# Latent attention in groups of two head columns, with its norms on GpSimd, in a two-block transformer kernel

## The reference, cut to what matters

```python
cq, ckv, kr, qd, kd, vd = _split(h @ w_in, CD_SIZES)
q = (rms_norm_2(cq, g_cq) @ w_uq).reshape(B, S, C_HEADS, C_NOPE + C_ROPE)   # 8 heads, 64 + 32
q_nope, q_rope = jnp.split(q, [C_NOPE], axis=-1)
q_rope = apply_rope_2(q_rope, ang_c)
kv = (rms_norm_2(ckv, g_ckv) @ w_ukv).reshape(B, S, C_HEADS, C_NOPE + C_V)
k_nope, v_c = jnp.split(kv, [C_NOPE], axis=-1)
k_rope = apply_rope_2(kr.reshape(B, S, 1, C_ROPE), ang_c)                   # one for all heads
qc = jnp.concatenate([q_nope, q_rope], axis=-1)[:, :, :, None, :]
kc = jnp.concatenate([k_nope, jnp.broadcast_to(k_rope, (B, S, C_HEADS, C_ROPE))], axis=-1)
oc = blocked_dense_attention(qc, kc, v_c, (C_NOPE + C_ROPE) ** -0.5)
...
s = jnp.einsum('bqhgd,bkhd->bhgqk', q_blk, k) * scale      # blocked_dense_attention, 128 queries a block
p = jax.nn.softmax(s, axis=-1)
return jnp.einsum('bhgqk,bkhd->bqhgd', p, v)
```

## Time and profile before

| what | value |
|---|---|
| median of 3 runs | 2272.75 us (2271.89 to 2274.1) |
| the profiled execution: its span | 2275.0 us |
| the profiled execution: its own run time | not given |
| instructions | 33281 |
| TensorE busy | 2199.9 us |
| VectorE busy | 1246.9 us |
| ScalarE busy | 1078.0 us |
| GpSimd busy | 853.7 us |

### The profile page before, as it was taken

One profiled execution on the slowest core, in us unless ns is written; L12 is line 12 of the kernel. 1 busy time (PEld: TensorE's weight loads), 2 busy tenths in 40 slices (PEclk: granted clock), 3 DMA queues, 4 the chain that ended last, 5 costly groups with the idle time before them and its releaser, 6 DMA issues.

```text
span 2275.0 us, 33281 instructions
## 1 busy us (share of the span) xinstructions
PE 2199.9 (97%) x12130; PEld 1763.7 (78%) x12130; DVE 1246.9 (55%) x2614; ACT 1078.0 (47%) x2160; POOL 853.7 (38%) x665
## 2 busy tenths in 40 slices
PE   8999899999999999989999999999999999999997
PEld 6778667888866788668888888888767888888886
DVE  6997782499778446885552112234666655211222
ACT  6542484465247652685453223343566545322332
POOL 4333304443330343104255545554110425554553
PEclk9999899999999999999999999999999999999998
DMA  5334002332410233203233333343110323333331
GB/s 171 85 91 141 25 2 79 104 91 79 144 38 11 75 89 109 68 2 110 67 94 96 95 109 98 92 124 95 48 60 20 111 66 97 94 95 100 98 96 66
DMA packets 107186, 189.74 MB, mean 83 GB/s; under 512 B 12049, under 2 KB 22801, under 8 KB 106897
## 3 DMA queue, kind: packets, MB, share of 16 engines
q1 hardware_dynamic: 101136, 178.67, 27.3%
q10 hardware_dynamic: 5888, 8.95, 1.2%
HBM read 182.85 MB, written 2.10 MB: 81 GB/s over the span
## 4 chain that ended last, share of the span: by engine, by line
PE 85%; DVE 10%; issue 3%; ACT 2%; POOL 1%; DMA 0%; SPq 0%; DVEq 0%; ACTq 0%
PE bank L861 23%; PE bank L863 23%; PE bank L862 23%; PE bank L1090 3%; PE bank L1103 3%; PE bank L1076 2%; DVE temp L1933 1%; DVE bank L2053 1%; PE bank L868 1%; DVE temp L1965 1%; PE bank L1067 1%; PE bank L1070 1%; PE bank L931 1%; DVE temp L1967 1%; POOL w_lo L2212 1%
## 5 line engine op out<-in xcount | busy, mean ns | idle before, releaser
L2212 POOL TENSOR_TENSOR w_lo<-w_raw,w_hi 128x512 fp32r<-128x512 f32 (+3 forms) x618 | 824.7, 1341 | 1337.1 <-ACT w_hi L1226 1336.7
L861 PE MATMUL bank<-op_hi,w_hi 128*128 128x512 f32 x1840 | 734.4, 399 | 9.1 <-POOL w_lo L2212 4.4
L863 PE MATMUL bank<-op_hi,w_lo 128*128 128x512 f32 x1840 | 719.4, 391 | 0.0
L862 PE MATMUL bank<-op_lo,w_hi 128*128 128x512 f32 x1840 | 719.4, 391 | 0.0
L1226 ACT ACTIVATE w_hi<-w_raw 128x512 fp32r<-128x512 f32 (+2 forms) x634 | 385.4, 617 | 682.5 <-PE bank L863 678.8
L861 PEld LDWEIGHTS bank<-op_hi,w_hi 128*128 128x128 f32 x1840 | 347.1, 189 | 95.7 <-issue 15.3
L862 PEld LDWEIGHTS bank<-op_lo,w_hi 128*128 128x128 f32 x1840 | 347.6, 189 | 73.4 <-issue 4.1
L863 PEld LDWEIGHTS bank<-op_hi,w_lo 128*128 128x128 f32 x1840 | 347.1, 189 | 73.7
L1648 DVE TENSOR_TENSOR temp<-bank,rstd 128x512 f32<-128x512 f32 x151 | 104.4, 691 | 396.0 <-PE bank L863 378.2
L861 PE MATMUL bank<-side_hi,w_hi 128*128 128x512 f32 (+1 forms) x628 | 233.2, 371 | 2.5 <-DVE side_lo L1730 1.4
L863 PE MATMUL bank<-side_hi,w_lo 128*128 128x512 f32 (+1 forms) x628 | 230.9, 368 | 0.0
(11 more groups left out here) (269 smaller groups left out, 2256.3 us busy)
## 6 DMA issues: line engine op xcount, KB each, us to landing
w_raw<-in_weights SPq DMA_DIRECT2D x620, 256.0 KB, 2.7
w_raw<-in_weights SPq DMA_DIRECT2D x32, 192.0 KB, 2.3
temp<-temp SPq DMA_DIRECT2D x40, 64.0 KB, 2.0
x_t<-in_x SPq DMA_DIRECT2D x8, 256.0 KB, 5.4
conv_area<-in_mem ACTq DMA_DIRECT2D x2, 1024.0 KB, 5.5
out_y<-ybuf SPq DMA_DIRECT2D x8, 256.0 KB, 2.1
conv_area<-in_bias ACTq DMA_DIRECT2D x1, 1920.0 KB, 8.0
conv_area<-in_bias ACTq DMA_DIRECT2D x2, 960.0 KB, 4.9
```

The source lines that it names most:

```text
L861: pe.matmul(dst, w[0], m[0], start=start, stop=False)
L862: pe.matmul(dst, w[0], m[1], start=False, stop=False)
L863: return pe.matmul(dst, w[1], m[0], start=False, stop=stop)
L2212: pool.tensor_tensor(w_lo[:, j, 0:n], w_raw[:, p % RAW_RING, 0:n], w_hi[:, j, 0:n].bitcast(F32), ALU.subtract).then_inc(*mark("weights_spl ...
```

## The change

C2 works in groups of two pairs: head columns j and j + 1 at one query block, four tiles in four score banks. The plain products are made pair by pair, then the rotated ones of the four tiles in each of three passes, at four quarters of 32 rows. At step s TensorE gives out scores of group s, values of group s - 2, turns of group s - 1. Turns use bank 4, bank 5, the group's own output bank, and bank 4 again. VectorE only inverts the sums; GpSimd scales the tile, a `tensor_scalar` with two scalars (the inverse and a one). Copies of tiles 1 and 3 go to VectorE.

In AB2, D2 and C2 the outputs of two query blocks (C2: of two head columns) share a bank, and are copied at once (a group of outputs has size 4). The first values of such a group wait for `copied(a + 2)` as well.

All stages score into banks 1, 2, 3, 0 from the start. The gate strip of NSA and the layer norm's small products go from bank 0 to bank 7; NSA's outputs use bank 6 only, each waiting for the one before. `E` has 8 buffers for 6, and the fourth `PT` is `rstd`, whose first copy in NSA waits for the gate strip. Extras stand at the end of a step, behind the norms on VectorE and the copies on ScalarE; only `split` keeps its lag. The gate strip's chunks come as 2, 2, 4 instead of 2, 1, 1, 4. NSA's three warm products are gone, AB2 has two in place of one. In C2 the last two splits come after the stage, and the drain is dealt out otherwise. GpSimd gets an `attend`, with the layer norm's squares at fixed steps of NSA, and two weight pieces' subtractions (`split_to`) at step 5 of a stage (step 2 of C2).

The diff, cut:

```diff
-TURN_LAG = 2
-VALUE_LAG = 3
+PAIRS = {"NSA": 1, "AB2": 1, "D2": 1, "C2": 2, "X2": 1}
+TURN_LAG = {1: 2, 2: 1}
+VALUE_LAG = {1: 3, 2: 2}
+NEXT_SPLIT = 10
+VECTOR_COPIES = (1, 3)
+LATE_LOWS = ("split",)
+E_RING = 8
+SCORES = (1, 2, 3, 0)
+GATE_CHUNKS = (2, 2, 4)
-WARM_TURN = {"NSA": {30: 3}, "AB2": {0: 1}, "D2": {0: 2}, "C2": {0: 2}, "X2": {0: 2}}
+WARM_TURN = {"NSA": {}, "AB2": {0: 2}, "D2": {0: 2}, "C2": {0: 2}, "X2": {0: 2}}
...
-            return bank[2 if n == 2 else 0 if n in LAST_GATE.values() else n % 2]
+            return bank[2 if n == 2 else 7 if n in LAST_GATE.values() else n % 2]
...
+                if kind == "C2":
+                    order = [(j + e, i) for j in (0, 2) for i in range(NT) for e in range(2)]
...
-                                            size=2, pos=r, width=HD, y=ybuf[:, yc, qs], chunks=[yc], qs=slice(0, P), start=True, stop=True))
+                                            size=4, pos=2 * half + r, width=HD, y=y, chunks=chunks,
+                                            qs=slice(P * half, P * half + P), start=True, stop=True))
...
+        PT = [tmp(E_RING), tmp(E_RING + 1), tmp(E_RING + 2), rstd[:, :]]
...
-                 "C2": ((0, 0), (0, 0, 0), (0, 1, 1), (1, 1, 1, 1, 0, 1)),
+                 "C2": ((0, 0), (0, 0, 0, 0, 1), (), (1, 1, 1, 1, 1)),
...
+                    t["out"], t["out_held"] = (6, at_group - 1) if step[1][0] == "NSA" else (6 + at_group % 2, at_group - 2)
+                    t["turn"] = 4 + n % 2
+                    if PAIRS[step[1][0]] == 2:
+                        third = t["out"] if step[1][0] != "NSA" else 7 if n >= LN_TILES else 4
+                        t["turn"] = (4, 5, third, 4 if third != 4 else 5)[n % 4]
...
+                def latent_scores(group):
+                    parts = ((0, 0), (0, 1), (1, 0))
...
+                    for pair in group:
+                        free_banks(pair)
+                        for x, y in parts:
+                            for t in pair:
+                                pe.matmul(score_bank(t), t["q"][x], t["k"][y], start=(x + y == 0), stop=False)
+                    for x, y in parts:
+                        for t in group[0] + group[1]:
+                            ins = pe.matmul(score_bank(t), t["more"][0][x], t["more"][1][y], start=False, stop=(x == 1))
...
                 def values(pair):
                     for t in pair:
-                        pe.wait_ge(*after("probs_copied", t["a"]))
-                        if t["first"] and t["g"] >= 2:
-                            pe.wait_ge(*after("outputs_taken", t["g"] - 2))
+                        pe.wait_ge(*copied(part, t["a"]))
+                        if t["first"] and t["out_held"] >= 0:
+                            pe.wait_ge(*after("outputs_taken", t["out_held"]))
+                        if t["first"] and t["size"] == 4:
+                            pe.wait_ge(*copied(part, t["a"] + 2))
...
+                    if scaled_by_pool(part, t):
+                        dve.reciprocal(total, total).then_inc(*mark("sums_inverted", a))
+                        return
...
+                def scaled(pair):
+                    t = pair[0]
+                    pool.wait_ge(*after("sums_inverted", pair[1]["a"]))
+                    total, _ = pair_sums(t)
+                    for r, t in enumerate(pair):
+                        e = E[t["a"] % E_RING][:, 0:t["nk"]]
...
+                            ins = pool.tensor_scalar(e, e, total[:, r:r + 1], C("ones")[:, 0:1], ALU.mult, ALU.mult)
+                        ins.then_inc(*mark("probs_scaled", t["a"]))
...
+                for s in range(steps_of(part)):
+                    if part[0] == "NSA" and s == 14:
+                        norm_squares(l, 0, 2)
+                    for pair in in_group(groups, s - 1):
+                        if scaled_by_pool(part, pair[0]):
+                            scaled(pair)
+                    if NEXT_SPLIT in moments_of(part, s):
+                        split_to(last_of(FOLLOWS[part] + 1))
```

More of the change, by code:

```diff
@@ L278, in build @@
         sp8 = sb("sp8", [P, 8])
-        small = sb("small", [P, 192])
+        small = sb("small", [P, 256])
         PAD = CONV_K - 1
@@ L600, in build @@
                     t["a"], t["g"] = at_tile, at_group
-                    banks = SCORES if step[1][0] == "NSA" and at_tile - ts[0]["a"] < LN_TILES else SCORES + (0,)
-                    t["bank"] = banks[(at_tile - ts[0]["a"]) % len(banks)]
+                    n = at_tile - ts[0]["a"]
+                    t["bank"] = SCORES[n % len(SCORES)]
                     t["held"] = held.get(t["bank"])
@@ L765, in score_bank, with grouped, by_vector, copied @@
             return bank[t["bank"]][:, 0:t["nk"]]
+        def grouped(part):
+            return PAIRS[part[0]] == 2
+        def by_vector(part, t):
+            return grouped(part) and (t["a"] - ATT[part][0]["a"]) % 4 in VECTOR_COPIES
+        def copied(part, a):
+            t = ATT[part][a - ATT[part][0]["a"]]
+            return after("probs_copied_vector" if by_vector(part, t) else "probs_copied", a)
+        def scaled_by_pool(part, t):
+            return grouped(part) and not t["cmp"]
         def tables_of(s):
@@ L1427, in copy @@
                     act.wait_ge(*after("probs_turned", a))
+                    if part[0] == "NSA" and a == ts[PT_RING - 1]["a"]:
+                        act.wait_ge(*taken(LAST_GATE[part[1]]))
                     if a >= PT_RING:
@@ L1972, in output @@
                     dve.wait_ge(*after("values", t["a"]))
-                    o = bank[6 + g % 2][:, 0:T if t["gate"] is not None else P if w == HD else 2 * P]
+                    o = bank[t["out"]][:, 0:T if t["gate"] is not None else 2 * P]
                     if t["gate"] is not None:
@@ L1978, in output @@
                     else:
-                        ins = dve.tensor_copy(t["y"], o if w == HD else o.rearrange("p (r q) -> p r q", r=2))
+                        ins = dve.tensor_copy(t["y"], o if len(t["chunks"]) == 1 else o.rearrange("p (r q) -> p r q", r=2))
                     ins.then_inc(*mark("outputs_taken", g))
-                for i in range(len(ts) + OUT_LAG + 1):
-                    if i == OUT_LAG + 3:
+                groups = groups_of(part)
+                _, value_lag = lags_of(part)
@@ L1984, in attend @@
+                for s in range(steps_of(part)):
+                    if NEXT_SPLIT in moments_of(part, s):
                         split_to(last_of(FOLLOWS[part] + 1))
-                    if i < len(ts):
-                        maxed(ts[i])
-                    if NORM_LAG <= i < len(ts) + NORM_LAG and i % 2 == 1:
-                        normed(ts[i - NORM_LAG:i - NORM_LAG + 2])
-                    if OUT_LAG <= i < len(ts) + OUT_LAG and ts[i - OUT_LAG]["last"]:
-                        output(ts[i - OUT_LAG])
@@ L1998, in extra_stage @@
+                    for i in moments_of(part, s):
+                        for stage in between.get(i - LOW_LAG[PAIRS[part[0]]], ()):
+                            if stage[0] in LATE_LOWS:
+                                extra_stage(*stage)
+                        for stage in between.get(i, ()):
+                            if stage[0] not in LATE_LOWS:
+                                extra_stage(*stage)
             def extra_stage(kind, l, c=None):
```

296 lines of the change are left out of this document (192 added, 104 removed).

## The result

The changed kernel takes 2284.49 us in the median of 16 runs, the kernel before 2276.94 beside it (2272.75 was the median of its first three). The ratio is 1.0034, 95% interval 1.002 to 1.0047: slower by a third of a per cent, 7.6 us, where 3.6 less was forecast. One execution took 4861.75 us; why isn't known, and it is left out of the ratio. The others lie between 2276.93 and 2292.68.

The account below looks back on a forecast made before the run. TensorE, busy 97% of the span, was taken to bound the kernel. C2 -6.5, AB2 +2.7, D2 +1.6 and NSA -1.4 summed to -3.6 us from the median 2272.75: 2269, range 2261 to 2279.

Parts of the forecast that it names:

- the price of the wait for `copied(a + 2)`: AB2 and D2: value products of every second pair wait 0.3 us; with other terms AB2 +2.7, D2 +1.6.
- B was to gain 0.3: B2, the VectorE-bound part of AB2: the wait is hidden there and output copies merged by two give -0.3 us.
- The warm product's +0.6: AB2: a second warm product before the first transposes, about 0.9 us, eats a following wait of 0.25: +0.6.
- The upper bound that I gave, +5: AB2: upper end of the +2.7 us estimate, with the wait in B2 exposed.
- four quarters share a pass: C2: rotated products of four tiles run together in passes of about 0.23 us, one set of three for two.
- the wait at `ln_factor`: NSA, each layer: extras move to the step's end, warm products go, a smaller wait comes at `ln_spread_factor`: -1.4 us.
- The -1.5 at 272: NSA, each layer: norms precede centring and PW's subtracts leave GpSimd, so a wait of 1.32 shrinks: -1.5, between 0 and -5.
- One output bank: NSA, each layer: with all outputs in bank 6, the next head's first value products wait for a copy: +1.1 us.
- the end, from NSA's last score product to the next mark: NSA, each layer: longer idle before the chunk awaiting ScalarE's silus, clock may drop: +1.1 us, between 0 and +3.
- Rival B: NSA keeps its clock, the half-clock stretch goes, 3 us a layer more gained: total 2263 us, chance 0.20.
- rival E: NSA's edges go wrong (bank 6, late end at half clock, 3 us a layer): 2275 to 2278 us, chance 0.12.
- D: C2: GpSimd is slow, 1.38 us a scaling, C2 +2.2 and total +5.1: 2278 us, chance 0.13.

Follow-up runs that it names:

- e1: The changed kernel, but value products wait for `copied(a + 2)` only in C2, where the bank is shared: 2272.27 us, ratio 0.9989.
- e2: The kernel before, with only the wait for the copy two tiles on added to value products in AB2 and D2: 2286.04 us, ratio 1.0047.
- e9: The changed kernel with the `copied(a + 2)` wait only in C2, one warm product in AB2, five before NSA's last drain: 2278.59 us, ratio 1.001.
- e6: The changed kernel with C2's norms on VectorE in place of GpSimd: 2285.31 us, ratio 1.0026.
- e3: The changed kernel with C2 in single pairs, norms on VectorE, copies on ScalarE, no `copied(a + 2)` wait in C2: 2285.07 us, ratio 1.0053.
- e11: The changed kernel as it is, run once more: 2284.22 us, ratio 1.0034 to the kernel before.
- e8: The changed kernel with VectorE's extras in NSA at even tiles ahead of the norms again: 2297.85 us in two runs, ratio 1.009.
- e7: The changed kernel with NSA's banks as before (three score banks for 44 tiles, outputs in banks 6 and 7): 2280.58 us, ratio 1.0018.
- e12: The changed kernel with NSA's three warm products back ahead of the transposes of tile 30: 2285.96 us, ratio 1.0037.
- e4: The changed kernel with C2's rotated products issued one pair after the other, two sets for one: 2282.73 us, ratio 1.0028.
- e5: The changed kernel with each C2 pair's rotated products right behind its own plain ones: 2289.35 us, ratio 1.0055.

## Why the prediction was wrong

**The step that failed is the price of the wait for `copied(a + 2)`,** +2.7 in AB2 and +1.6 in D2, where 6.49 and 3.16 were measured. The mechanism was named and is right: e1 takes it away and gets 5.4 and 3.3 us back, e2 adds it alone and loses 5.76 and 3.22. Its size was off by three terms. (1) I put the copied result at +1.3 behind the transposes' start and the value products at +1.0; they begin at +1.54, because the copy starts at +0.69, takes 0.60, and the products start 0.25 after its end, which I had left out: 0.5 a wait in place of 0.3, eight times in A and eight times in D. (2) The pair of AB2 in which ScalarE does four weight pieces was priced like the others; there the copy was queued behind 2.18 us of other work and the wait was 2.0, 1.4 us of it new. Looking up what ScalarE has ahead of each awaited copy would have found it. (3) B was to gain 0.3 and takes 0.6 more in e2. In D2 the part that bias scaling covers was about right (1.1 us in e2, 0.8 in the forecast). The warm product's +0.6 was right too (0.7, by e9). The upper bound that I gave, +5, was too low as well.

**How much of the miss that is.** Forecast was 3.6 us less and measured 7.6 more: 11.2 us between them. The wait gives 5.4 of it, NSA most of the rest (below). The 2269 itself lies 15.5 under the measured 2284.49, since I had also started from the 2272.75 of three executions, where 2276.94 was measured beside the changed kernel.

**C2** was right in sum, -6.80 for -6.5, and in most terms: groups of 6.32 for 6.25, start 1.7 and 0.3 idle for 1.6 and 0.6, p of 0.77 for 0.75, weight pieces 1.64 for 1.6. The assumption that four quarters share a pass holds. From the 3.07 of the Trainium skill (TensorE: Matmul & The Clock Gate, the table row on small-K matmuls) I had estimated 0.2 us more for each rotated set; the set took 0.90, as with two tiles, so here the trace disagrees. The 768 ns of the Trainium skill (GPSIMD Engine Reference, 3.1) agrees with the 773 measured. That GpSimd is the wrong choice for ordinary elementwise arithmetic, as the introduction of that page of the Trainium skill says, is so for one instruction (773 ns, VectorE 440), but not for the stage, by the groups of e6.

**NSA is the second sum that failed.** It was forecast at -0.7 a layer. In the seven traces with the changed kernel's NSA (after, e1, e3 to e6, e11) layer 0 averages +0.7 and layer 1 -0.5, but with less low clock in most of them than before. Against low clock, layer 0 goes from -1.0 (6.8 us of it) over +1.0 (13.7) to +5.0 (23.9), layer 1 from -1.2 (10.2) over -0.6 (13.7) to +2.9 (20.5). Read off these at the 17.1 us of the kernel before, NSA takes some 2.3 and 1.1 us more: an estimate of +3.4 for -1.4.

Term by term, in layer 0: the wait at `ln_factor` went as forecast, 3.3 us of warm products and idle time for a wait of 1.5, and e8 confirms that the order of the extras gained. The -1.5 at 272 didn't come. I had expected a wait of 1.32 to shrink; TensorE arrived 1.0 us sooner and waited 2.3, so the transposes start as long after NSA's first product as before (30.9 and 30.8 us). One output bank cost more than the four score banks gave (e7). And the end, from NSA's last score product to the next mark, takes 2.0 to 2.6 us more in the seven traces, forecast +1.1; in layer 1 it is at most 0.5 in six of them.

How long TensorE stays at the low clock differs from execution to execution of the same instructions: 6.8 to 23.9 us in layer 0. Rival B (the clock is kept) and rival E (it is lost) are both to be seen, in different executions, but B's gain of 3 us more a layer came in none of the seven.

**Between traces and medians.** The trace of after is 2.3 us above that of before, the medians 7.6. At a mean clock of 0.989 the kernel before takes 2277.0 (median of 34 runs), the changed one 2282.85 and 2283.41 in e11: 6 us. The marks give the same, -6.8 in C2, +9.65 for AB2 and D2, +3.4 as estimated for NSA, and -0.45 ahead of the first mark and behind the last: 5.8. Of 77 executions of the kernel before 67 have 0.988 to 0.990; those of the changed one lie from 0.983 to 0.993. The trace of after (0.991) was one of its better executions. Why the changed kernel's clock is spread wider stays open. The warm products' return doesn't mend it (e12, 0.985 to 0.992). With NSA's banks as before (e7) the eight executions lie closer together, 0.986 to 0.989, so the one output bank may have a part in it; but eight are few, and neither that nor the wait at 272 was taken away alone.

D (GpSimd is slow, 0.13) and E (NSA's edges, 0.12) had the right sign. D's mechanism isn't there (p is 0.77); E's is, in part: the output bank and the late end cost what is said above. No rival had the wait at its true price as the thing that turns the sign. With it the sum would have been +1.8 in place of -3.6.

## What to carry to other kernels

When a condition of one stage (here "size 4") comes to hold in others, count the wait in each of them, and price it from the queue of the engine that it waits for, other work included, not from the bare latency. In A, where TensorE is busy without a gap, the wait cost its full length every time; by the marks e1's one line is worth 8.7 us. Compare stage by stage with marks in the timeline before reading a total: a gain of 6.8 us and a loss of 9.7 lay side by side here, and the total of one trace showed neither. And where the granted clock moves between executions, compare a stage at the same time spent at the low clock: NSA looked level, and by the estimate above it wasn't.

## What was unexpected of the hardware

In C2, matmuls at different quarters of 32 rows overlapped even though they were issued a whole set of three passes apart (e4: starts within 0.024 us of each other, with six matmuls of the first pair issued ahead of the third start). So the order inside the set didn't matter; products of another shape between them did (e5: 1.1 us a group). And two `tensor_scalar` of VectorE from SBUF to SBUF took 2.75 us instead of 0.88 while GpSimd subtracted (e6), so that GpSimd, slower by the instruction (773 ns for 440), was the better place for them even in the two groups about the weight pieces, by 0.4 us.
